# A two-network decoder in split fp32: token tile 0 ahead of tile 1 at the block seams

## What is computed

```python
# first_block
mod = silu(c) @ w_ada + b_ada            # six vectors of 1024
h = modulate(rms_norm(x, g_mix), sh_m, sc_m)
proj = h @ w_in                          # two attentions of 8 heads, gates
x = x + gt_m * ((g_a * ya + g_b * yb) @ w_out)
h2 = modulate(rms_norm(x, g_ffn), sh_f, sc_f)
u = causal_depthwise_conv(h2 @ w_up)     # 3 taps
x = x + gt_f * ((gelu(u_gate) * u_val) @ w_down)
x = rms_norm(x, g_final)
# second_block, twice (l = 0 even mixer, l = 1 odd mixer)
x = x + 0.5 * rmsnorm(swiglu(rmsnorm(x, g0), wg, wu, wd), g1)
x = x + rmsnorm(mixer(rmsnorm(x, g2)), g3)
x = x + 0.5 * rmsnorm(swiglu(rmsnorm(x, g4), wg, wu, wd), g5)
```

## Time and profile before

| | |
|---|---|
| median of 3 runs | 1610.46 us (1610.44 to 1612.14) |
| span of the profiled execution | 1604.4 us; no other time of it is given |
| TensorE matmul busy | 1477.3 us, 92% |
| VectorE busy | 979.7 us, 61% |
| ScalarE busy | 728.7 us, 45% |
| GpSimd busy | 39.1 us, 2% |
| chain that ended last | TensorE 83%, VectorE 10%, ScalarE 3% |
| mean granted TensorE clock | 0.958 |

### The profile page before, as it was taken

One profiled execution on the slowest core, in us unless ns is written; L12 is line 12 of the kernel. 1 busy time (PEld: TensorE's weight loads), 2 busy tenths in 40 slices (PEclk: granted clock), 3 DMA queues, 4 the chain that ended last, 5 costly groups with the idle time before them and its releaser, 6 DMA issues.

```text
span 1604.4 us, 17772 instructions
## 1 busy us (share of the span) xinstructions
PE 1477.3 (92%) x6791; PEld 1215.7 (76%) x6791; DVE 979.7 (61%) x1305; ACT 728.7 (45%) x962; POOL 39.1 (2%) x79
## 2 busy tenths in 40 slices
PE   6999897799997999989788999989999899899997
PEld 5778785578885888867566888878888677688885
DVE  5675578666767555576865555575555645565554
ACT  1556532455555444355444444444443555454432
POOL 1000100000000000011100000000000100000000
PEclk9999798899998999999879999999999899999999
DMA  8963466455553655544313556546665653346551
GB/s 309 326 230 120 158 208 210 133 165 191 170 184 118 201 192 183 162 170 132 105 54 117 184 187 196 187 136 201 196 189 191 183 165 106 105 152 196 188 186 53
DMA packets 180292, 274.27 MB, mean 171 GB/s; under 512 B 6225, under 2 KB 120657, under 8 KB 180209
## 3 DMA queue, kind: packets, MB, share of 16 engines
q1 hardware_dynamic: 176960, 263.45, 50.4%
q0 software_dynamic: 1824, 6.57, 1.4%
q10 hardware_dynamic: 1425, 3.12, 0.6%
HBM read 272.05 MB, written 1.06 MB: 170 GB/s over the span
## 4 chain that ended last, share of the span: by engine, by line
PE 83%; DVE 10%; ACT 3%; issue 2%; DMA 2%; POOL 0%; SPq 0%; DVEq 0%; ACTq 0%
PE psum L1629 25%; PE psum L1631 24%; PE psum L1630 24%; DVE w_lo L1227 2%; PE psum L1821 2%; PE psum L1697 2%; DMA raw<-in_w_ada_dram 1%; PE psum L1751 1%; ACT w_hi L1036 1%; PE psum L1750 1%; DVE scr L1569 1%; PE psum L1766 1%; DVE ada_acc L1291 1%; PE psum L1789 1%; DVE X L1588 1%
## 5 line engine op out<-in xcount | busy, mean ns | idle before, releaser
L1227 DVE TENSOR_TENSOR w_lo<-raw,w_hi 128x2048 fp32r<-128x2048 f32 x227 | 517.7, 2287 | 296.9 <-ACT w_hi L1036 296.5
L1629 PE MATMUL psum<-w_hi,hT_hi 128*128 128x512 f32 x1376 | 550.3, 400 | 17.1 <-DVE hT_lo L1233 6.2
L1630 PE MATMUL psum<-w_lo,hT_hi 128*128 128x512 f32 x1376 | 539.4, 392 | 0.0
L1631 PE MATMUL psum<-w_hi,hT_lo 128*128 128x512 f32 x1376 | 539.3, 392 | 0.0
L1036 ACT ACTIVATE w_hi<-raw 128x2048 fp32r<-128x2048 f32 x227 | 432.1, 1907 | 220.8 <-PE psum L1631 183.1
L1629 PEld LDWEIGHTS psum<-w_hi,hT_hi 128*128 128x128 f32 x1376 | 261.8, 190 | 79.5 <-issue 14.3
L1631 PEld LDWEIGHTS psum<-w_hi,hT_lo 128*128 128x128 f32 x1376 | 261.4, 190 | 55.9
L1630 PEld LDWEIGHTS psum<-w_lo,hT_hi 128*128 128x128 f32 x1376 | 261.9, 190 | 51.6 <-issue 0.2
L1629 PE MATMUL psum<-w_hi,hc_hi 128*128 128x512 f32 x440 | 173.0, 393 | 6.1 <-DVE hc_lo L1233 4.9
L1631 PE MATMUL psum<-w_hi,hc_lo 128*128 128x512 f32 x440 | 172.3, 392 | 0.0
L1630 PE MATMUL psum<-w_lo,hc_hi 128*128 128x512 f32 x440 | 172.1, 391 | 0.0
(11 more groups left out here) (182 smaller groups left out, 1077.4 us busy)
## 6 DMA issues: line engine op xcount, KB each, us to landing
raw<-in_ffn_wg_dram SPq DMA_DIRECT2D x88, 512.0 KB, 4.0
raw<-in_ffn_wu_dram SPq DMA_DIRECT2D x88, 512.0 KB, 5.0
raw<-in_ffn_wd_dram SPq DMA_DIRECT2D x44, 1024.0 KB, 4.9
raw<-in_w_ada_dram SPq DMA_DIRECT2D x24, 1024.0 KB, 5.3
raw<-in_w_up_dram SPq DMA_DIRECT2D x44, 512.0 KB, 4.8
raw<-in_w_in_dram SPq DMA_DIRECT2D x20, 1024.0 KB, 5.3
raw<-in_even_w_in_dram SPq DMA_DIRECT2D x12, 1024.0 KB, 5.1
raw<-in_odd_w_in_dram SPq DMA_DIRECT2D x12, 1024.0 KB, 5.2
```

Of the source, the lines that this page charges most:

```text
L1227: nc.vector.tensor_tensor(unit_view(w_lo, s % SPLIT, s), unit_view(raw, raw_slot["w", s], s), unit_view(w_hi, s % SPLIT, s).bitcast(F32), ...
L1629: nc.tensor.matmul(o, a_hi, b_hi, start=start, stop=False)
L1630: nc.tensor.matmul(o, a_hi, b_lo, start=False, stop=False)
L1631: return nc.tensor.matmul(o, a_lo, b_hi, start=False, stop=stop)
```

## The change

1. At each seam the last products of the old layer are put in order by token tile: tile 0's are finished first, then `cross` lays the remaining products of tile 1 between the steps of tile 0's chain (squares, multiply, root, add, turn). After tile 1's last product come the first two half-layers of the next block for tile 0 alone, under which tile 1's chain runs; `go_on` then mixes the tiles and falls back to the old order. `pick`, `ts` and `ks` say which products a step holds. The end of the kernel is a seam without a next layer; its store is one per token tile.
2. In all turns but the modulated ones, and in the non-convolution `hturn`, ScalarE writes the rounded high half straight from PSUM, and VectorE subtracts it from PSUM for the low half. The cast and the buffer `turned` fall away there; the bank is free only after VectorE. At the seams a group is two column tiles of one token tile, two ScalarE and two VectorE instructions of 128 columns.
3. The reciprocal root is one GpSimd power, `v ** -0.5`, after one VectorE sum; the division by the width is in the scale of the squares.
4. The add to X is one instruction of 1024 columns per token tile. The gain row is loaded when the last sum of a seam is made, with no memset.
5. Weight splits are steps of their own (`split_hi`, `split_lo`), placed by hand at the seams and by `split_to` elsewhere.
6. In the convolution feed-forward the down steps lag by one chunk more at the end: chunk 9's turn follows its up products directly, and `down(8)`, half of `down(9)` and more stand behind chunk 10's turn.

The plan's part, cut to the core (`+` lines are new; `cross`, `go_on` and `tail`):

```diff
+    def cross(chain, head, pieces):
+        a, b = chain
+        a(0)
+        pieces[0]()
+        if head:
+            head.begin()
+            pl.hi_to(head.u0)
+        b(0)
+        pieces[1]()
+        if head:
+            pl.lo_to(head.u0)
+        pieces[2]()
+        if head:
+            pl.hi_to(head.u0 + 1)
+            head.turn(0, (0, 1))
+        else:
+            pl.add("store", t=0, after=x_at[0])
+        pieces[3]()
...
+        pl.lo_to(head.u0 + 1)
+        head.turn(0, (2, 3))
+        a(1)
+        head.mm(0, 0)
+        head.mm(1, 0)
+        pl.hi_to(head.u0 + 2)
+        b(1)
+        pl.lo_to(head.u0 + 2)
+        head.turn(1, (0, 1))
+        head.mm(2, 0)
+        head.turn(1, (2, 3))
+        head.go_on()
...
+        def go_on(self):          # FfnHead
...
+                self.st = x_stats(x_at)
+            self.mm(0, 1)
+            pl.split_to(us[3])
+            self.mm(1, 1)
+            pl.split_to(us[3] + 1)
+            self.out(0)
+            self.mm(3, 0)
+            self.mm(2, 1)
+            pl.split_to(us[3] + 2)
+            self.hidden_turn(0)
+            self.mm(3, 1)
+            self.out(1)
+            self.down(0)
+            self.hidden_turn(1)
...
+        def tail(self, chain, head):
+            c = NFC - 1
+            self.up(c, 0)
...
+            product_step("up", second, ts=(0,), inc=ups[0])
...
+            pl.split_to(self.downs[c])
+            self.out(c, (0,))
+            self.down_step(c - 1, self.halves(0, 0) + self.halves(0, 1), False)
+            self.hidden_turn(c, (0,), 6)
+            product_step("up", second, ts=(1,), ks=(0, 1), inc=None)
+            self.down_step(c, self.halves(0, 0) + self.halves(0, 1), False)
```

The engines' part:

```diff
@@ gpsimd
+                elif kind in ("var", "diffnorm"):
...
+                    nc.gpsimd.tensor_tensor(stat[:, st["r"][0] + i0:st["r"][0] + i1], v, minus_half[:, 0:i1 - i0], ALU.pow)\
+                        .then_inc(rstd_ready, 1)
@@ scalar
+            def turned_hi(a):
+                wait_past(act, a["free"])
...
+                    for i in range(a["nk"]):
+                        g = cols[:, a["scale"][1] + k0 + i:a["scale"][1] + k0 + i + 1]
+                        ins = nc.scalar.activation(tiles_of(hT_hi, k0 + i, 1, a["ts"])[:, 0, :],
+                                                   psum[:, a["use"].bank, i * w:(i + 1) * w], ACT.Copy, scale=g)
@@ vector
+            def split_lo(s):
...
+                if s >= SPLIT:
+                    dve.wait_ge(unit_used, s - SPLIT + 1)
...
+                        for i in range(nk):
+                            g = cols[:, a["scale"][1] + k0 + i:a["scale"][1] + k0 + i + 1]
+                            ins = nc.vector.scalar_tensor_tensor(lo[:, i, :], psum[:, use.bank, i * w:(i + 1) * w], g,
+                                                                 hi[:, i, :].bitcast(F32), ALU.mult, ALU.subtract)
...
+                elif kind == "post_add":
...
+                        dve.wait_ge(rstd_ready, a["st"]["r_at"][t])
+                        ins = nc.vector.scalar_tensor_tensor(X[:, t, :], scr[:, t, :], col(a["st"], "r", t), X[:, t, :],
+                                                             ALU.mult, ALU.add)
```

More of the change, by code:

```diff
@@ L251, in turn, with var, x_squares, tile_stat @@
                 w = after if j == 0 else None
[L252 to L261, removed]
+            turn_group(G, src, w, scale, bias, k0 + 2 * j, 2, (0, 1), banks[j % len(banks)])
+        return G
+    def var(st, ts, q, two, eps):
+        n = pl.var()
+        for t in ts:
+            st["r_at"][t] = n
+        pl.add("var", st=st, ts=ts, q=q, two=two, eps=eps, n=n)
+        return n
+    def x_squares(st, ts, after):
+        for t in ts:
+            q = pl.square()
+            pl.add("xsq", st=st, t=t, q=q, after=after[t])
+        return q
+    def tile_stat():
+        st = pl.new_stat(TT)
+        st["r_at"] = [0] * TT
+        return st
+    def x_stats(after):
+        st = tile_stat()
+        var(st, (0, 1), x_squares(st, (0, 1), after), False, EPS)
         return st
@@ L428, in build_plan, with down_step, down, up @@
-    rows_used = [0]
+                    self.y[b] = pl.use(b, by_unit=b == 3)
+        def down_step(self, c, pick, done):
+            pl.add("down", c=c, unit=self.downs[c], uses=self.y, gs=self.gs, pick=pick, done=done)
+        def down(self, c):
+            self.down_unit(c)
+            pl.split_to(self.downs[c] + LOOK)
+            self.down_step(c, [(k, t, half) for k in range(2) for t in range(TT) for half in range(2)], True)
+        def up(self, c, i):
+            if c not in self.units:
+                self.units[c] = self.up_units(c)
+            if i == 0:
+                self.open(c)
+            p = self.parts[c][i]
+            pl.split_to(p["unit"] + LOOK)
+            product_step("up", p)
@@ new lines, in go_on @@
+        def go_on(self):
+            us = [u for c in (0, 1) for u, _ in self.units[c]]
+            if not self.conv:
+                self.st = x_stats(x_at)
[12 more added lines that the diff above has]
+            self.hidden_turn(1)
+            for c in range(2, NFC - 1):
+                self.up(c, 0)
+                self.up(c, 1)
+                self.out(c)
+                if not (self.conv and c == NFC - 2):
+                    self.down(c - 1)
+                self.hidden_turn(c)
@@ L459, in build_plan @@
     pl.add("modfinal", vec=1, gain=0)
-    pl.add("prime", units=[0])
-    g0 = turn("scr", ("halves", scr_version(), scr_version()), ("mod", 1), ("mod", 0))
-    pl.add("prime", units=list(range(1, LOOK)))
+    pl.split_to(0)
+    G = turn("scr", ("halves", scr_version(), scr_version()), ("mod", 1), ("mod", 0))
+    pl.split_to(LOOK - 1)
     pl.add("late_loads")
@@ L1272, in _ @@
                                             ALU.add).then_inc(lam_dots, 1)
[L1273 to L1275 removed]
+                elif kind == "split_lo":
+                    split_lo(a["unit"])
                 elif kind == "ada":
```

911 lines of the change are left out of this document (538 added, 373 removed).

## The result

The change makes the kernel **slower by 0.35%**: 1613.8 us median of 20 runs (1609.8 to 1620.3) against 1609.2 us of 20 runs of the kernel before (1601.2 to 1612.1), ratio 1.0035, 95% interval 1.0026 to 1.0043. The forecast was 1603, its rival B 1615.

A forecast was written before the change was run, and what follows sets the result against it. TensorE, busy 92% of 1604.4 us, was the bound, with some 80 us to be had at the seams. Terms summed to -11.2 us, the clock added 4: span 1597.2, plus 6.1 gives 1603 us; range 1580 to 1618.

The forecast's parts named there:

- rival B: Behind tile 1's turns: short waits drop the clock inside blocks, 10 to 14 us over, 1615; chance 0.2.
- the clock term: Five seams with waits near 2.5 us close together: 0.8 us added for each, between 0 and 2: +4 us.
- One feed-forward seam: Seam at 1062 us: new waits of 8.1 us against old ones of 7.1, so 1.0 us lost.
- Odd projection: Seam into it: 4.0 us of waits left, against 9.4, 0.3 and 1.7 of slow products; 7.4 us gained.
- Behind attention: Seams at 873 and 1404 us: new waits 7.6 against 7.5 and 8.2, one cast less each; 1 us gained for both.
- First seam: Tile 1's chain and first hidden turn run later: first down product at 327.7 instead of 323.24; 4.4 us lost.
- The convolution's last chunk and the seam behind it: Last chunk 4.8 us gained as its 4.24 us wait and slow products go; seam to feed-forward 3.3 lost.
- The root: Ten VectorE steps, 2 us, become one GpSimd power, priced 0.5 us with both hand-overs, on the path twice a seam.
- Rival C: At tile 1 in every seam, tile 0 in five: power costs 1.3 us, 10 us more, 1612; chance 0.1.
- D: Seams: tile 0 not ahead in effect, waits only change place; within 3 us, 1610; chance 0.05.
- The small copies: Four 256-column ScalarE copies a seam become sixteen of 128, 0.65 us a group of two, bounds 0.5 and 0.84.
- A: Seven seams: queues overlap better than the ledger; half the new waits go, 25 us less, 1578; chance 0.2.

The follow-up runs named there:

- e5_root: Kernel before with only the root moved, from ten VectorE steps to one step and one GpSimd power: 1601.7 us, ratio 0.9969.
- e4_both: Changed kernel with tile 0's third block ahead of tile 1's turns and steps behind those turns reordered: 1568.8 us, ratio 0.9767 to the kernel before.
- e2_reorder: Changed kernel with the steps behind tile 1's turns in another order, no work added or removed: 1576.7 us, ratio 0.9807 to the kernel before.
- e1_filler: Changed kernel with eight overwritten products in each of two waits of five heads: 1605.2 us, ratio 0.9981 to the kernel before.
- e9_filler4: Changed kernel with four overwritten products in each of two waits of five heads: 1603.5 us, ratio 0.9982 to the kernel before.
- e7_root_direct: Kernel before with the root as GpSimd power and high halves written straight from PSUM, without the skew: 1597.3 us, ratio 0.9937.

## Why the prediction was wrong

**The step that failed is the clock term**, "I add 0.8 for each, between 0 and 2: +4". The slow count rose by 14.6 us in the profile pair, and the ledger had already taken off 4.0 of slow products of before (2.3 behind the convolution's last chunk, 1.7 before the odd projection), so the term to set beside the 4 is 18.6. With it the sum is -11.2 + 18.6 = +7.4, against +10.7 measured. If 4 to 6 us of it are the luck of this pair, as estimated above, the term is 13 to 15 for a median run, over three times what was put down, and the sum +1 to +3, against +4.6 in the medians. The mechanism is rival B's: "several short ones can drop it in the middle of a block". B counted 14 drops of 2 us, "perhaps half of them real"; fourteen came in this profile, of 1.5 us on average. It is also the sign that the prediction named for B, the lower clock inside blocks. The error was to draw a small term per seam from one row behind a single 2.5 us wait, while the ledger itself listed three waits of 1.75 to 2.3 us in every seam, each with its own chance of a drop.

The Trainium skill (TensorE: Matmul & The Clock Gate, HAM oscillation) has the rule that was cited for B, that bursts broken by waits each start cold. The traces agree as to the loss, and differ twice. Not every wait is followed by slow products: of the ten that were later filled, seven are. And they rarely begin at once: most begin 0.3 to 1.5 us after the wait, in the row above 1.2 (1098.86 to 1100.1).

The other terms of the sum, from the two profiles. Each is the difference of the stretch, then the same less the slow count of the changed kernel in it, which is what the ledger's term was for:

- **One feed-forward seam**, forecast +1.0: +4.2, less 3.2 is +1.0. The four late waits are the ledger's within some 0.2 us. The sum is exact partly by luck: of the 1.15 us of early waits only 0.19 came, and each wait costs some 0.2 us more than its idle time, since products that follow one another start before the last has ended, which the ledger left out.
- **Odd projection**, -7.4: -6.6, less 1.3 is -7.9. **Even projection**, -2.2: -1.0, less 2.0 is -3.0. **End**, -2.5: -3.8. **Attention**, -2: -2.3.
- **Behind attention**, two seams, -1: +5.9, less 4.7 is +1.2, so 2.2 worse.
- **First seam**, +4.4: +11.3, less 5.5 is +5.8. The first down product came at 331.40, not 327.7.
- **The convolution's last chunk and the seam behind it**, -1.5 together: +4.3, less 4.0 is +0.3. The last chunk's wait, which was to go, is still 1.49 us.

These miss by 2.2 us at most and by 2.5 in sum, with misses of both signs. Apart from the clock the ledger holds.

**The root** was priced at 0.5 us with both hand-overs. The power alone takes 0.55 to 0.73, and VectorE idles 0.88 for it [e5_root]. Rival C's 1.3 is ruled out. So is D, since tile 0 is ahead: its transposes wait for nothing in this seam. **The small copies** are 0.37 us each by their own duration, but ScalarE starts one every 0.25 us (four from 1091.09 to 1092.10), so a group of two is 0.5 to 0.6 instead of 0.65. The Trainium skill's figure (VectorE: DVE Perf Modes, errata section) gave an estimate of 0.25 us: the distance of the starts agrees with it, the duration of one does not.

**A**, that the queues overlap better than the ledger, is out for the change itself; but its 25 us were there to be had. They needed two changes of order, not better overlap (e4_both).

**What stays open**: which short wait drops the clock. The same pair of waits (0.9 and 1.57 us) was followed by slow products in the change and in e2_reorder (1064.0, six products) but not in e1_filler and e9_filler4. And a kernel with e7_root_direct's edits and the skew alone was not run; the 16 us are a difference of two measured ratios and hold the change's other edits too.

## What to carry to other kernels

A wait of 1.5 to 2.5 us on TensorE can cost as much again in the products behind it; when a change splits one long wait into several short ones, count the waits, not their sum, and price each with a drop. When a ledger names the waits that are left, reorder for them before the change is judged: here the same edits gave 1.0035 or 0.9747 by the order of a few steps. Where a wait can't be removed, a few products into a free bank keep the clock, but they are the lesser cure: 0.5% here, against 2.9% for taking most of the waits away.

## What the runs showed of the hardware that I had not expected

- Filling products pay although they compute nothing: 0.9 us of work in each of ten waits (eight of 2.1 us, the convolution's two of 1.8 and 6.35) is worth 8.5 us of a 1614 us kernel by the ratios, and twice as many are worth no more.
- The drop can come late: 1.2 us into a block that runs at full speed the products slow down, the granted clock from 1100 to 1103.5 is 0.52, and full speed comes back with TensorE busy throughout.
- Shortening a long wait by 0.95 us gave 0.2 us in the seam at 1062 us, since its slow stretch ran on into the products behind.
- Two runs of one kernel differ mostly by the clock: the change's twenty spans go from 1608 to 1619 us as the mean granted clock goes from 0.967 to 0.959.
- GpSimd's power: 545 ns for one column, 728 ns for two, and 0.88 us of idle time on VectorE with both hand-overs.
